# Four convolution taps moved to two other engines, the top-k mask drawn ahead, and the last stores split over two queues

## The reference

```python
u = h @ w_in
cv, cg, cs, lx, ls = split(u)                    # 1024 columns each
v = cv * sigmoid(cg)
v = causal_depthwise_conv(v, dw_w, dw_b)         # 31 taps per channel
v = silu(layernorm(v)) @ pw2_w + pw2_b
y_conv = v * silu(cs)
xs = causal_depthwise_conv(lx, sc_w, sc_b)       # 4 taps
# r, i: sigmoids of block-diagonal products of xs; a = exp(-8 r softplus(-lam))
hs = linear_scan(a, sqrt(1 - a * a) * i * xs)
y = concat(y_conv, hs * silu(ls)) @ w_out
x = rmsnorm(x + (1 + gate) * y) * final_g
```

```python
_, idx = top_k(score, 128)      # per query, causal
p = softmax(q_lat . c_kv[idx] * scale - slope * dist)
```

## Time and profile before

| | us |
|---|---|
| median of three runs | 1070.28 |
| the profiled execution, its own time | 1071.27 |
| its span, first to last instruction | 1069.5 |
| PE busy | 1039.6 |
| DVE busy | 636.5 |
| ScalarE busy | 406.0 |
| GpSimd busy | 442.9 |

### The profile page before, as it was taken

One profiled execution on the slowest core, in us unless ns is written; L12 is line 12 of the kernel. 1 busy time (PEld: TensorE's weight loads), 2 busy tenths in 40 slices (PEclk: granted clock), 3 DMA queues, 4 the chain that ended last, 5 costly groups with the idle time before them and its releaser, 6 DMA issues.

```text
span 1069.5 us, 14024 instructions
## 1 busy us (share of the span) xinstructions
PE 1039.6 (97%) x5222; PEld 839.1 (78%) x5222; DVE 636.5 (60%) x1247; ACT 406.0 (38%) x561; POOL 442.9 (41%) x155
## 2 busy tenths in 40 slices
PE   7999999999999999999999999999999999699997
PEld 5787796667878888888888888888887778588886
DVE  5377995976463422234256111789999999864322
ACT  4244335784242212122142321422136786262242
POOL 0034342592333534435344534144354565524350
PEclk9999999999999999999999999999999999899999
DMA  9993231140424345343472332233322223212312
GB/s 326 349 297 118 72 109 40 41 159 1 157 79 157 118 151 163 119 155 118 161 242 89 109 109 79 79 117 120 111 86 79 79 79 105 92 40 86 111 40 79
DMA packets 127251, 128.92 MB, mean 121 GB/s; under 512 B 3552, under 2 KB 125280, under 8 KB 127200
## 3 DMA queue, kind: packets, MB, share of 16 engines
q1 hardware_dynamic: 126240, 127.90, 36.8%
q10 hardware_dynamic: 960, 0.34, 0.1%
HBM read 126.13 MB, written 2.10 MB: 120 GB/s over the span
## 4 chain that ended last, share of the span: by engine, by line
PE 49%; issue 33%; POOL 10%; DVE 5%; DMA 1%; SPq 1%; ACT 1%; POOLq 0%; DVEq 0%; ACTq 0%
PE bank L680 11%; PE bank L682 10%; PE bank L681 10%; POOL w_lo L578 9%; DVE bank L2108 2%; PE bank L997 1%; PE bank L1026 1%; PE bank L869 1%; PE bank L1178 1%; DMA ada_stage<-in_w_ada 1%; PE bank L1220 1%; PE bank L1221 1%; PE bank L1222 1%; PE bank L887 1%; PE bank L705 1%
## 5 line engine op out<-in xcount | busy, mean ns | idle before, releaser
L578 POOL TENSOR_TENSOR w_lo<-w_stage,w_hi 128x2048 fp32r<-128x2048 f32 x78 | 366.9, 4704 | 538.5 <-ACT w_hi L1291 538.5
L680 PE MATMUL bank<-act_hi,w_hi 128*128 128x512 f32 x848 | 335.8, 396 | 0.5 <-POOL w_lo L578 0.5
L682 PE MATMUL bank<-act_hi,w_lo 128*128 128x512 f32 x848 | 330.0, 389 | 0.0
L681 PE MATMUL bank<-act_lo,w_hi 128*128 128x512 f32 x848 | 330.0, 389 | 0.0
L1291 ACT ACTIVATE w_hi<-w_stage 128x2048 fp32r<-128x2048 f32 x78 | 149.3, 1914 | 245.8 <-PE bank L682 235.7
L680 PEld LDWEIGHTS bank<-act_hi,w_hi 128*128 128x128 f32 x848 | 159.2, 188 | 38.1 <-issue 6.3
L681 PEld LDWEIGHTS bank<-act_lo,w_hi 128*128 128x128 f32 x848 | 159.2, 188 | 33.8 <-issue 1.9
L682 PEld LDWEIGHTS bank<-act_hi,w_lo 128*128 128x128 f32 x848 | 159.2, 188 | 33.5
L2108 DVE SCALAR_TENSOR_TENSOR bank<-v_pad,vcol,bank 128x512 f32<-128x512 f32 x232 | 153.9, 745 | 0.0
L2024 DVE TENSOR_TENSOR tmp<-bank,tmp 128x512 f32<-128x512 f32 x22 | 15.2, 692 | 157.0 <-PE bank L682 153.6
L680 PE MATMUL bank<-ff_hi,w_hi 128*128 128x512 f32 x176 | 69.7, 396 | 0.0
(11 more groups left out here) (306 smaller groups left out, 1485.2 us busy)
## 6 DMA issues: line engine op xcount, KB each, us to landing
w_stage<-in_w_in SPq DMA_DIRECT2D x29, 1024.0 KB, 5.1
w_stage<-in_w_gu SPq DMA_DIRECT2D x22, 1024.0 KB, 5.1
ada_stage<-in_w_ada SPq DMA_DIRECT2D x20, 1024.0 KB, 11.6
w_stage<-in_w_out SPq DMA_DIRECT2D x12, 1024.0 KB, 5.1
ada_stage<-in_mod_w SPq DMA_DIRECT2D x12, 1024.0 KB, 7.6
w_stage<-in_w_down SPq DMA_DIRECT2D x8, 1024.0 KB, 5.2
late_stage<-in_w_ada SPq DMA_DIRECT2D x4, 1024.0 KB, 8.8
w_stage<-in_pw_w SPq DMA_DIRECT2D x4, 1024.0 KB, 5.1
```

Of the source, the lines that this page charges most:

```text
L578: nc.gpsimd.tensor_tensor(w_lo[b][:], w_stage[b][:], w_hi[b][:].bitcast(F32), ALU.subtract).then_inc(s_lo, 1)
L680: pe.matmul(dst, wh, rhs_hi(k), start=(first and k == 0), stop=False)
L681: pe.matmul(dst, wh, rhs_lo(k), start=False, stop=False)
L682: mm = pe.matmul(dst, wl, rhs_hi(k), start=False, stop=(last and k == n_k - 1))
```

## The change

Tiles 2 to 7 (`k >= 2`) give away taps 0 to 3. For each pair of tiles ScalarE writes tap 0 with its bias to `conv` and the products of taps 1 to 3 to six buffers that are free at this time (`tap_products`). GpSimd adds the six in place to `conv` (`add_taps`), and DVE begins with tap 4, which takes that sum from SBUF as its third operand. DVE's portions keep their counts, with 224 instructions instead of 248 in the list. `tap_products(1)` and `(2)` stand at the head of ScalarE's third and fourth pass, `(3)` behind the fourth; the passes are written out instead of looped. `add_taps` stands behind the low parts of chunks `C_IN2` + 5, 7 and 9.

In the attention the search stops six steps before its end (`TOP_TAIL = 6`) instead of twelve, the first minimum follows, then the six mask steps; none is left in the ticks. ScalarE rounds chunk `C_OUT + 1` in front of the copy of the turned unit 2 instead of behind it. Of the eight stores SyncE issues six, and ScalarE the last two odd ones, behind its last two scalings.

```diff
-TOP_TAIL = 12
+TOP_TAIL = 6
+AWAY = 4
+def taps_away(k):
+    return AWAY if k >= 2 else 0
+        tap_bufs = [tmp[2], tmp[3], decay[0], decay[1], hidden[0], rstd]
# SyncE
-            for s in range(2 * TT):
-                half, t = divmod(s, TT)
+            for half, t in ((0, 0), (0, 1), (0, 2), (0, 3), (1, 0), (1, 2)):
...
-            sp.wait_ge(s_out, 16 * 2 * TT)
+            sp.wait_ge(s_out, 16 * 6)
+            sp.wait_ge(s_outodd, 16 * 2)
# GpSimd
-            lo_loop(C_GU, first_y)
+            def add_taps(p):
+                for n in range(2, 2 * AWAY):
+                    k = 2 * p + n % 2
+                    pool.wait_ge(s_tap, 2 * AWAY * (p - 1) + n + 1)
+                    if n >= 4:
+                        pool.wait_ge(s_tapsum, (2 * AWAY - 2) * (p - 1) + n - 3)
+                    nc.gpsimd.tensor_tensor(conv[:, k, :], conv[:, k, :], tap_bufs[n - 2][:], ALU.add).then_inc(s_tapsum, 1)
+            lo_loop(C_GU, C_IN2 + 4)
+            for n in range(C_IN2 + 4, first_y):
+                lo(n, n % 2)
+                if n in (C_IN2 + 5, C_IN2 + 7, C_IN2 + 9):
+                    add_taps((n - C_IN2 - 3) // 2)
# ScalarE, attention
+                if tick == 3:
+                    hi_part(C_OUT + 1, (C_OUT + 1) % 2, (C_OUT + 1) // 2)
                 if TURN_LAG <= tick < N_U + TURN_LAG:
                     turned(tick - TURN_LAG)
...
-                if tick == 3:
-                    hi_part(C_OUT + 1, (C_OUT + 1) % 2, (C_OUT + 1) // 2)
# ScalarE, second block
-            with act.Fori(0, KD // 2) as j:
+            def tap_products(p):
+                for n in range(2 * AWAY):
+                    k, tap = 2 * p + n % 2, n // 2
+                    src, w = v_pad[:, k, tap:tap + T], col("dw_w_2", 8 * tap + k)
+                    act.wait_ge(s_v, 2 + k + 1)
+                    if tap == 0:
+                        nc.scalar.activation(conv[:, k, :], src, ACT.Identity, scale=w, bias=col("dw_b_2", k)).then_inc(s_tap, 1)
+                    else:
+                        if p >= 2:
+                            act.wait_ge(s_tapsum, (2 * AWAY - 2) * (p - 2) + n - 1)
+                        nc.scalar.activation(tap_bufs[n - 2][:], src, ACT.Copy, scale=w).then_inc(s_tap, 1)
+            for j in range(KD // 2):
+                if j >= 2:
+                    tap_products(j - 1)
...
+            tap_products(KD // 2 - 1)
# ScalarE, first gate of the LRU part
+                    if k == 0:
+                        act.wait_ge(s_tapsum, (2 * AWAY - 2) * (KD // 2 - 1))
# ScalarE, end
+            for t in range(1, TT, 2):
+                act.wait_ge(s_on, TT // 2 + t // 2 + 1)
+                nc.scalar.dma_start(out[t * P:(t + 1) * P, D // 2:D], o_nat[:, t, D // 2:D]).then_inc(s_outodd, 16)
# VectorE
             least_of(0)
+            top_steps(TOP_TAIL)
...
-                if tick >= 2:
-                    top_steps(1)
...
-            taps = [... for tap in range(CONV) for k in (2 * p, 2 * p + 1)]
+            taps = [... for tap in range(taps_away(2 * p), CONV) for k in (2 * p, 2 * p + 1)]
...
-                    if tap == 0:
+                    if tap > 0 and tap == taps_away(k):
+                        dve.wait_ge(s_v, 2 + k + 1)
+                        dve.wait_ge(s_tapsum, (2 * AWAY - 2) * (k // 2) - 1 + k % 2)
+                        V.scalar_tensor_tensor(acc, src, w, conv[:, k, :], ALU.mult, ALU.add).then_inc(s_conv, 1)
+                    elif tap == 0:
...
-            dve.wait_ge(s_conv, CONV * KD)
+            dve.wait_ge(s_conv, len(taps))
```

More of the change, by code:

```diff
@@ L385, in build @@
         s_conv = sem("conv_step")
+        s_tap = sem("tap_product")
+        s_tapsum = sem("tap_product_added")
         s_xs = sem("short_conv_step")
@@ L420, in build @@
         s_out = sem("out_stored")
+        s_outodd = sem("last_odd_rows_stored")
         block = ctx.enter_context(nc.Block())
@@ L2092, in _ @@
             V.memset(l_pad[:, :, 0:PADL], 0.0).then_inc(s_v, 1)
-            taps = [(k, tap) for p in range(KD // 2) for tap in range(CONV) for k in (2 * p, 2 * p + 1)]
+            taps = [(k, tap) for p in range(KD // 2) for tap in range(taps_away(2 * p), CONV) for k in (2 * p, 2 * p + 1)]
             taps_done = [0]
```

## The result

The changed kernel takes 1064.9 us (median of 5 runs, 1064.7 to 1065.4) beside 1070.28 for the kernel before in the same session (5 runs, 1070.05 to 1072.34): ratio 0.9945, 95% interval 0.9934 to 0.9956. It is faster, but by 5.4 us and not by the 9.4 forecast; 1064.9 lies outside the range given (1057.3 to 1063.8). Its profiled execution took 1064.87, with a span of 1063.1 (before: 1071.27 and 1069.5).

The account below looks back on a forecast made before the run. TensorE, busy 97% of the span, was taken as the bound, plus its waits and slow clock. -10.8 + 2.1 + 0.5 - 1.2 = -9.4 us gave 1061.9 against the profiled execution, 1060.9 for the median; range 1057.3 to 1063.8.

Parts of the forecast that it names:

- The gap and the slow clock at the mean: At the convolution mean's product: TensorE's 8.2 us wait and 2.6 us of slow clock both go, -10.8 us.
- The additions at 1.29: GpSimd's 18 added tap additions: 1.29 us each, bounds 1.2 and 2.13.
- the first two bursts: GpSimd's first two groups of six additions: the low parts behind them stay hidden from TensorE, by 2.4 us.
- rival (3): In-place additions in the convolution cost 2.13 us each and eat the gain, 1071.3 us; chance 0.05.
- The stores: Last eight stores, two now from ScalarE's queue: transfer engines are full, so 0 (-0.5 to +0.5).
- The attention: Mask steps moved, conversion in front: 3.0 us gain, partly lost to a blocked copy, third spread at 203.9; -1.2 us.
- the third burst: At the short convolution: GpSimd stands during VectorE's stream, TensorE waits for the tenth chunk's low part; +2.1 us (0 to 4).
- The joining taps: First taps taking GpSimd's sum: delayed 2.6 and 2.8 us behind low parts, hidden by VectorE's idle time; 0, at most 1.5.
- +0.5: After the last scan: VectorE's first L2169 may delay GpSimd's last LRU instruction and TensorE; +0.5 us (0 to 0.6).
- the correction from the profiled execution to the median: Whole kernel: the profiled execution, 1071.27 us, lay 1.0 above the median 1070.28, so forecast 1061.9 became 1060.9.
- Rival (2): Attention gives nothing or loses 1, joining taps lose 1 to 2 more: 1063.6 us; chance 0.22, up to 1066.

Follow-up runs that it names:

- mask_only: The kernel before with the attention's mask steps moved alone, the weight chunk's conversion left behind the turned copy: 1069.22 us, ratio 0.9990.
- idle_burst: The kernel after, with all six GpSimd additions of the third burst waiting for three steps of VectorE's short convolution: 1071.01 us, ratio 1.0004.
- late_burst: The kernel after, with the third burst of GpSimd's additions one chunk later, behind chunk C_IN2 + 10's low part: 1061.36 us, ratio 0.9915.
- dve_late: The kernel before with 36 instead of 26 taps ahead of the LRU's gates, nothing else: 1063.55 us, ratio 0.9931.
- two_pairs: The kernel after, with only tiles 2 to 5 giving taps away, no third burst or third joining pair: 1060.48 us, ratio 0.9906.
- dve_first: The kernel after, with the third burst's fifth GpSimd addition waiting for three steps of the short convolution: 1064.83 us, ratio 0.9947.

## Why the prediction was wrong

**Right.** The gap and the slow clock at the mean: -10.8 forecast; 8.16 and 2.57, 10.7 measured. The additions at 1.29: pairs take 2.53 to 2.56, and the first two bursts stay hidden (no addition takes rival (3)'s 2.13). The stores: nothing. The attention: -1.2 forecast, -1.04 measured, with the copy at 3.46 and its wait of 1.61 where they were expected, and the third spread at 204.06 in the chain of waits (forecast 203.9); but as mask_only shows, that sum is right by luck, by two errors that cancel: a gain taken at 3.0 that is 1.64, and a price of 1.8 (first spread at 187.1 instead of 185.29) that is 0.65 to 0.69.

**Wrong: the third burst.** The step said that GpSimd stands while DVE's short convolution streams and that PE waits 2.1 us for the low part at the tenth chunk, and it had no term for a loss of DVE. The reverse came: GpSimd kept going, no wait at the tenth chunk, and DVE lost 6.6 us. I had taken the rule from the low part at 778.15, which came from idle into a stream under way. In the kernel after, GpSimd is at work on the third burst when the stream begins. The step's arithmetic holds where its premise does: in idle_burst GpSimd stands, and the low part is late.

**Wrong: what DVE's lateness costs.** The joining taps stood at 0 because "DVE idles for ScalarE's gates". It does, but between 780 and 905 its busy time was 120.8 of 125 us: 4.2 of idle, a number I could have read and set against the sum of the delays. (The joining taps alone would have fitted: they cost DVE 1.34 and 1.05 us, not the 2.6 and 2.8 I had in mind.) A late scan holds ScalarE's next gates (`tmp` and `decay` are freed by it), and these hold PE. An estimate from these rows is DVE's delay less 4.2, and 0.6 for a low part for which PE then waits as well (L704; 0.56 to 0.59 in each kernel with such a delay):

```
            delay of DVE                      less 4.2  + 0.6   gate to mean over 126.53
after       6.6 + (2.75-1.41) + (2.46-1.41) = 9.0   4.8    5.4   5.37
late_burst  (3.49-1.41) + (4.07-1.41)       = 4.7   0.5    1.1   1.82
dve_late    10 x 0.665                      = 6.65  2.4    3.0   3.04
two_pairs   0                                       0      0     0.54 (the wait at the mean)
```

It gives after and dve_late within 0.05 us and late_burst 0.7 too low; there DVE kept 1.2 of its idle time (busy 123.8 of the same 125 us), so the idle time isn't all used up before PE pays. The sum is a rough rule, and not more. Nor do PE's waits add up to the whole: in the kernel after those between the cuts are 3.5 and 0.6, 4.1 of the 5.37, and the other 1.3 the trace puts down to no wait.

The terms +2.1, 0 and +0.5 are thus one term of +5.4: 2.8 us of the miss. Attention and gap add 0.2. The last 1.0 is the correction from the profiled execution to the median: before's lay 1.0 above its median, after's (1064.87) lies on it. The range failed with the same step: I had priced the collision only as GpSimd's loss (0 to 4), and DVE's loss at the same place was no case of its own. Rival (2), with 1063.6, came nearest. The reason given there, that DVE is full from 810 on, holds; its other half, an attention that gives nothing or loses 1, did not come, so that the number is near is in part luck.

## What to carry to other kernels

When two engines exclude each other, price the collision once with each of them as the one that stands; the trace of before shows only the order of arrival that it had. Before a delay is called hidden by idle time, add up the idle time of the stretch and all delays that draw on it: here 4.2 us against 9.0. And before work is moved to another engine to open a gap at the end, try to move it along its own: ten taps shifted ahead by one constant brought 7.4 us, and the whole change, with four taps of six tiles given away, 5.4.

## What the runs showed of the hardware

Where VectorE instructions with two operands in SBUF met GpSimd's, who stood was settled for more than one instruction. A stream of VectorE that began while GpSimd was idle kept it out to its end: 2.7 us at 778.15 before, and in the kernel after 5.0 us behind eight such steps and the two that follow them:

```profile
813.74 9.62 POOL L589 TENSOR_TENSOR w_lo<-w_stage,w_hi 128x2048 fp32r<-128x2048 f32 x1 [10.25 <-ACT w_hi L1315]
```

One that began while GpSimd was at work stood behind GpSimd's instructions, 6.6 us in the kernel after, and GpSimd lost 0.2 to 0.5 an instruction. Whether the start of the stream or the length of GpSimd's idle time ahead of its arrival decides, the runs don't show. Even a copy of one operand stood for most of a low part: 3.46 us instead of 0.43 for L1974; and the two steps L2180 of one operand each, beside the additions, took 2.22 instead of 1.00. The Trainium skill, page "SBUF — State Buffer", section "Who interferes with whom", has "Issue order, not op shape, decides who blocks". The runs agree that the shape doesn't decide: an addition of the same form stands in idle_burst and gets in in dve_first. The order of arrival doesn't tell these two apart either, since in both GpSimd came when VectorE's stream was under way.
